# Transposing probabilities and gated results by VectorE squares and a DRAM round trip, with scores a unit sooner and value products last

## The reference

```
h = RMSNorm(x) * gain;  proj = h @ w_in                       # (256, 9296)
A, 8 heads of 128: s = qa.ka / sqrt(128) + rel_bias[clip(q - k)],  masked by chunk of 64
B, 8 heads of 128: per query the top 64 keys by an indexer score; s = qb.kb / sqrt(128) - slope*|q - k|
p = softmax(s);  o = p @ v                                    # per head, keys summed
y = concat(o_A * silu(g_A), o_B * silu(g_B))                  # (256, 2048)
x = x + y @ w_out;  out = RMSNorm(x) * final_gain
```

## Time and profile before

| | |
|---|---|
| median of 3 runs | 533.94 us |
| the profiled execution: its time, its span | 533.62 us, 531.5 us |
| around the span | 2.12 us |
| TensorE busy, VectorE, ScalarE | 522.9 us, 351.5 us, 262.6 us |
| granted TensorE clock, mean | 0.997 |
| bytes moved | 102.45 MB, mean 193 GB/s |

### The profile page before, as it was taken

How to read it: one execution, slowest core, us unless ns; L and a number is a source line. 1 busy time by engine, 2 the same in 40 slices (tenths; PEclk the granted TensorE clock), 3 DMA queues, 4 the chain that set the end, 5 groups by cost and what they waited for, 6 DMA issues and landing times.

```text
span 531.5 us, 8164 instructions
## 1 busy us (share of the span) xinstructions
PE 522.9 (98%) x2791; PEld 451.4 (85%) x2791; DVE 351.5 (66%) x514; ACT 262.6 (49%) x381; POOL 28.1 (5%) x46
## 2 busy tenths in 40 slices
PE   8999999999999999999999999999999999999994
PEld 6899998888888888888888888888888888888883
DVE  5897785665767657668565767657576666756454
ACT  6875544444444344446363636354545444634342
POOL 1004043150000000000000000000000000000000
PEclk9999999999999999999999999999999999999998
DMA  8966976657555655654655554555444574765614
GB/s 287 382 202 194 287 221 199 188 177 275 179 186 187 195 199 196 190 187 140 198 161 164 180 165 158 166 171 179 158 158 159 181 267 150 232 200 186 204 45 158
DMA packets 60375, 102.45 MB, mean 193 GB/s; under 512 B 3504, under 2 KB 45376, under 8 KB 60096
## 3 DMA queue, kind: packets, MB, share of 16 engines
q1 hardware_dynamic: 58656, 96.68, 56.1%
q0 software_dynamic: 1264, 5.00, 3.2%
q10 hardware_dynamic: 432, 0.47, 0.3%
HBM read 99.24 MB, written 2.11 MB: 191 GB/s over the span
## 4 chain that ended last, share of the span: by engine, by line
PE 98%; DVE 0%; ACT 0%; DVEq 0%; issue 0%
PE acc L426 27%; PE acc L391 16%; PE acc L393 16%; PE acc L392 16%; PE acc L424 13%; PE aux L609 1%; PE aux L499 1%; PE acc L429 1%; PE acc L460 1%; PE aux L613 1%; PE aux L588 1%; PE aux L598 1%; PE aux L670 1%; PE acc L436 1%; PE aux L586 0%; PE aux L585 0%
## 5 line engine op out<-in xcount | busy, mean ns | idle before, releaser
L984 DVE TENSOR_TENSOR w_lo<-w_raw,w_hi 128x1024 fp32r<-128x1024 f32 x172 | 213.5, 1244 | 150.4 <-ACT w_hi L713 149.5
L713 ACT ACTIVATE w_hi<-w_raw 128x1024 fp32r<-128x1024 f32 x172 | 181.9, 1059 | 224.0 <-PE acc L393 111.0
L426 PE MATMUL acc<-acts,w_hi 128*128 128x512 f32 (+1 forms) x640 | 215.6, 387 | 0.0
L424 PE MATMUL acc<-acts,w_lo 128*128 128x256 f32 (+1 forms) x600 | 165.5, 276 | 0.0
L391 PE MATMUL acc<-w_hi,acts 128*128 128x512 f32 x376 | 148.1, 394 | 0.0
L393 PE MATMUL acc<-w_hi,acts 128*128 128x512 f32 x376 | 146.6, 390 | 0.0
L392 PE MATMUL acc<-w_lo,acts 128*128 128x512 f32 x376 | 146.3, 389 | 0.0
L426 PEld LDWEIGHTS acc<-acts,w_hi 128*128 128x128 f32 x640 | 119.0, 188 | 20.2
L424 PEld LDWEIGHTS acc<-acts,w_lo 128*128 128x128 f32 x600 | 113.4, 189 | 0.7
L393 PEld LDWEIGHTS acc<-w_hi,acts 128*128 128x128 f32 x376 | 70.6, 188 | 15.0
L392 PEld LDWEIGHTS acc<-w_lo,acts 128*128 128x128 f32 x376 | 70.7, 188 | 14.1
(11 more groups left out here) (169 smaller groups left out, 361.7 us busy)
## 6 DMA issues: line engine op xcount, KB each, us to landing
w_raw<-w_blocks SPq DMA_DIRECT2D x140, 512.0 KB, 3.7
w_raw<-wo_blocks SPq DMA_DIRECT2D x32, 512.0 KB, 3.6
w_raw<-w_blocks SPq DMA_DIRECT2D x8, 256.0 KB, 5.8
v<-x POOLq DMA_DIRECT2D x1, 2048.0 KB, 10.1
qk<-xT SPq DMA_DIRECT2D x7, 256.0 KB, 6.2
o<-ext_dram POOLq DMA_DIRECT2D x1, 1024.0 KB, 7.4
fgain<-final_gain POOLq DMA_DIRECT2D x1, 1024.0 KB, 8.2
out<-o SPq DMA_DIRECT2D x2, 512.0 KB, 3.0
```

The source lines that it names most:

```text
L424: nc.tensor.matmul(acc[:, bank:bank + n], w_lo4[:, u % RING, q, c], a_hi[:, k, tokens], start=False, stop=False)
L426: last = nc.tensor.matmul(whole, w_hi4[:, u % RING, q, c], acts[:, k, :, tokens], start=(k == 0), stop=(k == KT - 1))
L713: nc.scalar.activation(flat(w_hi[:, s, :, :]), w_raw[:, s, :], ACT.Copy).then_inc(hi_done, 1)
L984: nc.vector.tensor_tensor(flat(w_lo[:, s, :, :]), w_raw[:, s, :], flat(w_hi[:, s, :, :]).bitcast(f32), ALU.subtract).then_inc(lo_done, 1)
```

## The change

- TensorE's 48 transposes of p and 32 of y go. VectorE transposes p in squares of 32x32 (`turn_p`), right after `split_lo` 6, from SBUF to SBUF (`p_sq`). A square's place within the 128 partitions stays as it was, so SP then moves the squares: four stores into `p_dram`, one for each group of 32 partitions, and one fetch into `pT`, 3 KB a partition. In `pT[p, t, s]` the slot s (one of six 128x128 tiles) is innermost.
- y goes the same way, chunk by chunk: `turn_y`, four stores into `y_dram`, one fetch back into `o`. Chunks 0 to 2 are turned one block after they are gated, chunk 3 right after it is gated.
- SP does this between the loads of the next block (`turning`): `store_p` after load 1, `fetch_p` and `store_y` after load 3, `fetch_y` after load 6; chunk 3's store after the last load of block 18, its fetch after load 1 of block 19.
- `score_pair` comes after unit 1, `value_pair` after unit 7, the bias and maxima ahead of `split_lo` 6, the exps after `split_hi` 6.
- Gating lies between `split_lo` 12 and 13. `y_hi` and `y_lo` read `o` in SBUF, in two instructions each, most of them in block 17. The copies `pT1_out` and `pT0_out` go.

```
+        p = sb("p", [P, SLOTS * P])
+        p_sq = sb("p_sq", [P, QUADS, SQ, SLOTS])
+        pT = sb("pT", [P, P, SLOTS])
...
+        p_squares = p_sq[:, :, :, :].rearrange("p j c s -> p s j c")
...
+            def store_p(pair):
+                sp.wait_ge(p_turned, pair + 1)
+                for i in range(QUADS):
+                    sp.dma_start(p_dram[:, i, :].rearrange("(j r) x -> r j x", r=SQ),
+                                 p_sq_flat[i * SQ:i * SQ + SQ, :, :]).then_inc(p_stored, 16)
+
+            def fetch_p(pair):
+                sp.wait_ge(p_stored, (16 * QUADS) * pair + 16 * QUADS)
+                sp.dma_start(pT[:, :, :].rearrange("p t s -> p (t s)"),
+                             p_dram.rearrange("p i x -> p (i x)")).then_inc(pT_landed, 16)
...
+            def turning(units, pair, chunk=None):
+
+                for u in units:
+                    if u == 1:
+                        store_p(pair)
+                    if u == 3:
+                        fetch_p(pair)
+                        if chunk is not None:
+                            store_y(chunk)
+                    if u == 6 and chunk is not None:
+                        fetch_y(chunk)
...
+            turning(out_block(G_OUT, 0), 7, 2)
+            store_y(3)
+            for u in out_block(G_OUT + 1, 1):
+                if u == 1:
+                    fetch_y(3)
...
+            def value_pair(pair):
+                pe.wait_ge(pT_landed, 16 * pair + 16)
+                pe.wait_ge(aux_read[3], pair + AUX3_PAIRS)
                 for h in range(2):
                     for kt in range(TM):
...
+                        nc.tensor.matmul(aux[3][:, h * HD:h * HD + HD], pT[:, :, 2 * h + kt],
                                          v_flat[:, ds(place(pair, kt) + h * HD, HD)],
                                          start=(kt == 0), stop=(kt == TM - 1))
...
-                for u in range(3):
+                for u in range(2):
                     feature_unit(g, u, 0)
                 score_pair(i, 2 * i + 1)
-                feature_unit(g, 3, 0)
+                for u in range(2, 4):
+                    feature_unit(g, u, 0)
                 both_out(4)
                 pe.wait_ge(feat_out, 2 * g - 8)
-                feature_unit(g, 4, 0)
-                feature_unit(g, 5, 0)
-                transpose_pair(i, i + AUX23_B)
-                feature_unit(g, 6, 0)
-                value_pair(i, i + AUX23_B, i + AUX23_B)
-                feature_unit(g, 7, 0)
+                for u in range(4, UNITS):
+                    feature_unit(g, u, 0)
+                value_pair(i)
...
             for u in range(UNITS):
                 pe.wait_ge(ylo_done, u + 1)
                 unit(G_OUT, u)
-                if u + 3 < UNITS:
-                    y_transposes(u + 3)
...
+            def turn_p(pair):
+
+                dve.wait_ge(exp_done, 2 * pair + 1)
+                nc.vector.transpose(p_squares[:, 0:4, :, :],
+                                    p[:, 0:4 * P].rearrange("p (s j r) -> p s j r", s=4, j=QUADS))
+                dve.wait_ge(exp_done, 2 * pair + 2)
+                nc.vector.transpose(p_squares[:, 4:SLOTS, :, :],
+                                    p[:, 4 * P:SLOTS * P].rearrange("p (s j r) -> p s j r", s=2, j=QUADS)
+                                    ).then_inc(p_turned, 1)
...
+            gate_block(G_OUT - 1, 3, 2)
             y_lo(0)
...
+            outputs(7)
+            for m in range(TM):
+                gated(G_OUT - 1, 3, m)
+                dve.wait_ge(y_stored, 3 * 16 * QUADS)
+                dve.wait_ge(y_done, 7 + m)
+                last = turn_y(3, m)
+            last.then_inc(y_turned, 1)
+            split_lo(G_OUT, 3)
+            y_lo(4)
+            split_lo(G_OUT, 4)
+            y_lo(5)
+            split_lo(G_OUT, 5)
+            split_lo(G_OUT, 6)
+            y_lo(6)
+            y_lo(7)
+            split_lo(G_OUT, 7)
```

More of the change, by code:

```diff
@@ L33 @@
 MASKED = -1e30
+SQ = 32
+QUADS = P // SQ
+SLOTS = 6
 NOT_ADMITTED = -1e38
@@ new lines, in fetch_p, with store_y @@
+            def fetch_p(pair):
+                sp.wait_ge(p_stored, (16 * QUADS) * pair + 16 * QUADS)
+                sp.dma_start(pT[:, :, :].rearrange("p t s -> p (t s)"),
+                             p_dram.rearrange("p i x -> p (i x)")).then_inc(pT_landed, 16)
+            def store_y(chunk):
+                sp.wait_ge(y_turned, chunk + 1)
+                for i in range(QUADS):
+                    sp.dma_start(y_dram[ds(chunk, 1), :, i, :].rearrange("o (j r) x -> (o r) j x", r=SQ),
+                                 y_sq[i * SQ:i * SQ + SQ, :, :]).then_inc(y_stored, 16)
@@ new lines, in _ @@
+            with sp.Fori(2, G_VB) as g:
+                for u in feature_block(g, g - 1):
+                    pass
+            with sp.Fori(G_VB, G_VA) as g:
+                for u in token_block(g, g - 1):
+                    pass
+            for u in token_block(G_VA, G_VA):
+                pass
+            for u in feature_block(G_QKA, G_QKA):
+                pass
+            with sp.Fori(G_QKA + 1, G_GATE) as g:
+                turning(feature_block(g, g), g - (G_QKA + 1))
+            with sp.Fori(G_GATE, G_GATE + 2) as g:
+                turning(token_block(g, g), g - (G_QKA + 1))
@@ L329, in _ @@
+            with sp.Fori(G_GATE + 2, G_OUT) as g:
+                turning(token_block(g, g), g - (G_QKA + 1), g - (G_GATE + 2))
+            turning(out_block(G_OUT, 0), 7, 2)
[3 more added lines that the diff above has]
+                    fetch_y(3)
+            with sp.Fori(G_OUT + 2, G_END) as g:
+                for u in out_block(g, g - G_OUT):
+                    pass
             for n, (m, c) in enumerate(VECTOR_PARTS):
@@ L656, in _ @@
                 gate_block(g, i)
[L657 to L677, removed]
             both_out(token_count(G_OUT - 2))
@@ L899, in gate_block @@
                 split_hi(g, 6)
-                split_hi(g, 7)
                 exps(i + 4, False)
[L902 to L906, removed]
+                for c in range(7, 10):
+                    split_hi(g, c)
+                stage_q(q_next, q_next + 4, 8)
                 split_hi(g, 10)
@@ L1340, in _, with turn_y, gate_block @@
             feature_attention(3, True, 0, 4)
-            def gate_block(g, i):
-                split_lo(g, 6)
+            def turn_y(i, m):
+                chunk = o_flat[:, ds(i * (TM * CB) + m * CB, CB)]
+                return nc.vector.transpose(y_squares[:, m, :, :, :],
+                                           chunk.rearrange("p (k j r) -> p k j r", k=4, j=QUADS))
+            def gate_block(g, i, turned):
                 bias_a(i)
                 maxima(i + 4, False)
+                split_lo(g, 6)
+                turn_p(i + 4)
                 split_lo(g, 7)
-                split_lo(g, 8)
-                pT1_out(i + 4)
-                split_lo(g, 9)
-                split_lo(g, 10)
-                outputs(i + 4)
-                if not (isinstance(i, int) and i == 3):
-                    stage_rest(i + 1, i + 5, i + 5)
+                if turned is not None:
+                    if turned > 0:
+                        dve.wait_ge(y_stored, 16 * QUADS * turned)
+                    dve.wait_ge(y_done, 2 * turned + 2)
+                    turn_y(turned, 0)
+                    turn_y(turned, 1).then_inc(y_turned, 1)
+                split_lo(g, 8)
             def gated(g, i, m):
@@ L1364, in gated, with gate_end @@
                 nc.vector.scalar_tensor_tensor(ob, t_gate[:, m, :], 1.0, ob, ALU.add, ALU.mult).then_inc(y_done, 1)
-            with dve.Fori(0, 3) as i:
-                g = i + G_GATE
-                gate_block(g, i)
-                split_lo(g, 11)
-                for m in range(TM):
-                    gated(g, i, m)
+            def gate_end(g, i):
+                for c in range(9, 12):
+                    split_lo(g, c)
+                outputs(i + 4)
+                stage_rest(i + 1, i + 5, i + 5)
@@ L1381, in _ @@
-            gate_block(G_OUT - 1, 3)
+                for k in range(UK * q, UK * q + UK):
+                    last = nc.vector.tensor_tensor(a_lo[:, k, :].rearrange("p (m i c) -> p m i c", m=TM, i=QUADS),
+                                                   yT(q // 2, k % 4),
+                                                   a_hi[:, k, :].bitcast(f32).rearrange("p (m i c) -> p m i c", m=TM,
+                                                                                        i=QUADS), ALU.subtract)
@@ L1382, in _ @@
+                last.then_inc(ylo_done, 1)
+            gate_block(G_OUT - 1, 3, 2)
             y_lo(0)
-            gated(G_OUT - 1, 3, 0)
             y_lo(1)
-            gated(G_OUT - 1, 3, 1)
-            split_lo(G_OUT, 3)
+            split_lo(G_OUT, 1)
             y_lo(2)
             y_lo(3)
-            for q in range(4, 8):
-                y_lo(q)
-                split_lo(G_OUT, q)
+            split_lo(G_OUT, 2)
```

(2 more changed lines are left out.)

169 lines of the change are left out of this document (80 added, 89 removed).

## The result

The changed kernel takes 546.9 us (median of 4 runs) against 533.8: ratio 1.0239, 95% interval 1.0227 to 1.025. It is slower by 13.1 us; 526.0 had been predicted and the range ended at 536.9. Its profiled execution took 547.21 us, its span is 544.8.

The account below looks back on a forecast made before the run. TensorE was taken to bound the kernel. Transposes gone (-8.9 us) plus a junction stall (+1.0) gave -7.9, from 533.94 to 526.0 us; range 524.9 to 536.9, the likeliest case's own 524.9 to 528.

Parts of the forecast that it names:

- What bounds the kernel: Whole kernel: TensorE, busy 522.9 of 531.5 us; other engines and queues run in its shadow.
- what the transposes are worth: 80 transposes leave TensorE at 0.111 us each: 8.9 us gained in full.
- Value products only change place: Value products at each block's end: same 1.34 us in 12 passes despite the 24-byte step; 0 taken, bounds 0 to 10.8.
- the rival's own signs: Signs of strided weights in value products: weight loads near 0.30 us and 12 passes in 2.7 us.
- A rival with a chance of 0.25: Strided weights double each of 96 value passes, 0.22 us instead of 0.112: 536.8 us, chance 0.25.
- pT in time: Each block's value products: pT lands 1.1 to 2.1 us before needed, costing nothing; late-pT rival 529 to 538, chance 0.10.
- The 6.7 us into the block: VectorE's split before the bias starts 6.7 us into a block, ends at 7.9; the bias follows.
- Held loads cost nothing: Loads 2, 3 and 4 held on SP for 2 to 3 us; 2 us of room left, so no cost.
- The junction: First output block: chunk 3 of y arrives late for unit 6, stalling TensorE 1.0 us, bounds 0 to 5.
- v<-x: The 2 MB load of x slows chunk 3's round trip; rival: stall of 4 to 6 us, 530, chance 0.09.
- the one rival with no waits: Strided weights: slower value passes with no wait anywhere, 536.8 us, chance 0.25; the range reached to 536.9.
- Strided weights: Value products read pT with a 24-byte step; doubled passes add 10.8 us, chance 0.25; milder penalty 530 to 531.5, chance 0.06.

Follow-up runs that it names:

- the version without losses: Changed kernel with contiguous pT copy, preparation a block sooner, load 2 first, x in four pieces, chunk 3's stores and fetch ahead of loads: 525.31 us, ratio 0.9841.
- 10.6 alone: Kernel before, only the layout of pT changed so that value products read every sixth word: 544.33 us, ratio 1.0199.
- 9.6 in place: The 525.31 us version without ScalarE's copy, with the changed kernel's squares and strided pT: 534.94 us, ratio 1.0025.
- fetch first: Changed kernel with fetch_p right behind the stores after load 1, ahead of held loads 2 and 3: 543.66 us.
- load 2 first: Changed kernel with load 2 issued before SP waits for the squares, then stores and fetch of p, load 3 behind: 541.76 us.
- the order alone: Changed kernel with chunk 3's stores ahead of block 18's last load and its fetch ahead of block 19's loads, x in one piece: 542.69 us.
- x alone: Two runs of the changed kernel: x loaded only after chunk 3 of y is fetched, 545.42 us; x in four 512 KB pieces, 545.06 us.

## Why the prediction was wrong

- **What bounds the kernel; what the transposes are worth.** Right. 80 x 0.111 = 8.9 us was predicted; the version without losses gained 8.6, with blocks of 24.83 and 24.36 us where 24.73 and 24.38 stood.
- **Value products only change place: this step failed first.** The term was taken as 0 from bounds of 0 to 10.8, by contiguous loads that could say nothing of a step. It measured 10.6 alone and 9.6 in place; the upper bound, from the spacing of the passes and the column time of the rows, was right to 0.2 us, and the rival's own signs came (loads near 0.30 and 12 passes in 2.7 us were named; 0.314 and 2.56 to 2.91 were measured). A rival with a chance of 0.25 should have been the forecast: the earlier trace rows had shown no room for the load. The rule of the Trainium skill (SBUF — State Buffer, section Door 1: The DMA port swizzle) was the only evidence on a step, and it held.
- **pT in time: wrong for the first pair, and too close in the gate blocks.** The 6.7 us into the block were read off the second block and taken for all. The first bias starts at 244.57 in the earlier trace rows, after the preparation; the block began at 257.2 - 25.4 = 231.8, so that is 12.8 us in, and in the new order 11.6 instead of the 7.9 that was forecast. The row was used for a duration and not for its place. In the other pairs the chain came as forecast up to VectorE's transposes (the first store is issued 13.6 us into a feature block and 13.9 into a gate block; 13.4 and 13.7 were forecast), though the larger transpose took 1.16 us instead of 0.69 (near the upper bound; it writes with the same step). Behind them two errors offset each other by luck: the last store landed after 1.9 us instead of 3.3, the fetch after 5.4 instead of 3.4 to 4.1. About 1.0 was left in a feature block (279.7 + 5.4 = 285.1 against 286.1). A gate block had less, since the prediction held its landing too against the 23.4 us of a feature block, while by the earlier trace rows a gate block's units and scores end 25.04 - 1.34 - 0.66 = 23.0 us in: nothing was left in three of four, 0.8 us in all.
- **Held loads cost nothing.** As priced for the loads themselves; but they are released in front of the fetch and make it slow: 5.4 us behind them, 2.9 ahead of them (fetch first, load 2 first).
- **The junction.** The place was right, 1.0 us was too little: the wait was 3.5 us, within the bounds of 0 to 5. From the end of the last value product the order was: turned at 5.3 (forecast 5.1), split done at 6.5 (6.3), last store issued at 9.7 (8.1), stores landed at 13.4 (11.5 to 13), fetch at 18.3 (15 to 17), unit 6 started at 19.9 (17 to 18.5) where TensorE was ready at 16.4 (16.7). The sum had every leg, but the stores' issues and the fetch too short. (The 0.61 us of a gating step is 0.69 in the earlier trace rows; that moves nothing.) SP's order made most of the wait (4.2 us less for the order alone; 1.5 and 1.8 less, within the spread, for x alone), where the prediction had put it on v<-x.
- **What was not in the sum at all:** the half clock behind a wait. At the first pair a wait of 3.4 us cost 5.0 in all, at the junction one of 3.5 cost 6.5. The sum priced waits at their length.
- **The range** ended at the one rival with no waits. Strided weights and the waits were priced as alternatives; they add: 526.0 + 10.6 - 1.0 + 12.0 = 547.6, against 546.9 measured.

## What to carry to other kernels

Before an operand of TensorE gets a new layout, look at its step in bytes. Here weight loads already set the pace of the passes; with float32 words 16 bytes apart or more they took 318 to 324 ns instead of 189, the passes came 0.21 to 0.24 us apart instead of 0.112, and VectorE's write with a step of 24 bytes took 1157 ns instead of 688. When work is moved to a DMA round trip, place its issues in the queue by what is held behind and what is released in front of them; here the order on SP alone was worth 4 to 5 us in each of two places. Check the first and the last instance of a repeated stage, and each kind of block, for themselves. And price a wait of TensorE with the slow clock that may follow it: here waits of 3.4 and 3.5 us cost 5.0 and 6.5.

## What the runs showed of the hardware

- Weight loads of 128 float32 columns: 189, 197, 258, 324, 319 and 318 ns for steps of 1 to 6 words; steps 4 to 6 took the same at a clock of 0.558 (325, 318 and 318).
- VectorE's transpose in 32x32 squares, 512 elements a partition: 0.69 to 0.71 us into runs of 32 words, 1.16 to 1.17 when it writes with a step of 24 bytes (256 elements: 0.43 and 0.66). ScalarE's copy of 256 elements out of PSUM: 364 ns contiguous, 671 with the step.
- Four stores of 96 KB are issued in 1.8 us and the last lands 1.9 us after its issue; a fetch of 384 KB lands after 2.9 us with no load issued just ahead of it and after 5.4 behind two loads of 512 KB.
- TensorE's granted clock behind a wait, over all these executions. Behind each of the eleven waits of 2.9 to 4.2 us it went to 0.50, for 3.4 us in six cases and for 6.8 in five. Of the six waits of 2.0 to 2.7 us four were followed by it and two not (2.0 in one version, 2.7 in another); behind waits of up to 1.5 us it stayed at 1.00. The same wait of 3.4 to 3.6 us at the first pair had 6.8 us of it in most versions and 3.4 in one, so a microsecond or two between two runs can be that alone.
